# The rotary part of the attention scores in fp32r halves stacked on 128 rows, the queries' second half first, the sample's unit second in a head

## What is computed

```
q = (cq @ w_uq).reshape(B, T, B_HEADS, B_D_NOPE + B_D_ROPE)      # 8 heads, 128 + 64
q_nope, q_rope = q[..., :B_D_NOPE], _rope(q[..., B_D_NOPE:], pos)
q_lat = jnp.einsum('bthn,chn->bthc', q_nope, w_uk)
s = jnp.einsum('bthc,bsc->bhts', ql, kv_lat) + jnp.einsum('bthr,bsr->bhts', qr, kv_rope)
s = s.astype(f32) * ATTN_SCALE
s = jnp.where((k_pos[None, :] <= qp[:, None])[None, None], s, -jnp.inf)
p = jax.nn.softmax(s, axis=-1)
return jnp.einsum('bhts,bsc->bthc', p.astype(kv_lat.dtype), kv_lat)
```

## Time and profile before

| | us |
|---|---|
| three runs | 2582.6, 2584.0, 2591.3; median 2584.0 |
| the profiled execution | 2582.5 |
| its span, first to last instruction | 2580.7 |
| mean granted clock of TensorE over the span | 0.927 |

### The profile page before, as it was taken

The page is one execution under the profiler, slowest core; times in us unless marked ns, Lnnn a source line. Parts: engine busy times, 40 slices in busy tenths (PEclk is TensorE's granted clock), DMA queues, the critical chain, the costliest instruction groups (busy, mean ns, idle before and its releaser), DMA issues. The chain is left out here.

```text
span 2580.7 us, 39435 instructions
## 1 busy us (share of the span) xinstructions
PE 2296.5 (89%) x11502; PEld 1682.2 (65%) x11502; DVE 1370.6 (53%) x2344; ACT 1068.0 (41%) x1818; POOL 309.6 (12%) x390
## 2 busy tenths in 40 slices
PE   5999997878949999999698999999989399999976
PEld 3766665656737788788376666656667287788751
DVE  3213211557975655656384443434369765755647
ACT  2211212533135655655252444544331265654645
POOL 0000001550000100000010334000000010100103
PEclk8999997778969999999899999999999699999985
DMA  6456655536147867876645544222351387866856
GB/s 256 154 202 213 214 187 168 160 99 213 42 156 256 313 217 254 296 265 217 207 157 190 187 159 158 91 93 90 99 205 42 128 302 278 296 243 222 307 183 222
DMA packets 193987, 499.26 MB, mean 193 GB/s; under 512 B 19360, under 2 KB 39297, under 8 KB 187392
## 3 DMA queue, kind: packets, MB, share of 16 engines
q1 hardware_dynamic: 163838, 401.76, 46.0%
q0 software_dynamic: 18992, 66.20, 7.1%
q10 hardware_dynamic: 11058, 30.06, 3.1%
HBM read 432.41 MB, written 68.70 MB: 194 GB/s over the span
## 5 line engine op out<-in xcount | busy, mean ns | idle before, releaser
L1952 DVE TENSOR_TENSOR e_wl<-e_raw,e_wh 128x1024 fp32r<-128x1024 f32 x384 | 449.3, 1219 | 96.4 <-ACT e_wh L1863 95.1
L1863 ACT CAST e_wh<-e_raw 128x1024 fp32r<-128x1024 f32 x384 | 382.3, 1048 | 103.4 <-DMA e_raw<-in_e_up 45.2
L1782 PE MATMUL e_psG<-e_wh,e_xh 128*128 128x512 f32 x784 | 321.5, 410 | 10.2 <-issue 7.4
L1784 PE MATMUL e_psG<-e_wh,e_xl 128*128 128x512 f32 x784 | 311.7, 398 | 0.0
L1783 PE MATMUL e_psG<-e_wl,e_xh 128*128 128x512 f32 x784 | 310.2, 396 | 0.0
L1782 PE MATMUL e_psY<-e_wh,e_hh 128*128 128x512 f32 x392 | 160.8, 410 | 28.2 <-DVE e_hl L1975 28.2
L573 PE MATMUL in_ps<-in_w_upper,in_h_upper 128*128 128x512 f32 (+1 forms) x432 | 174.8, 405 | 3.6 <-issue 3.6
L1782 PEld LDWEIGHTS e_psG<-e_wh,e_xh 128*128 128x128 f32 x784 | 148.7, 190 | 42.6 <-issue 8.2
L1784 PEld LDWEIGHTS e_psG<-e_wh,e_xl 128*128 128x128 f32 x784 | 148.3, 189 | 36.9
L1783 PEld LDWEIGHTS e_psG<-e_wl,e_xh 128*128 128x128 f32 x784 | 149.1, 190 | 32.0
L574 PE MATMUL in_ps<-in_w_lower,in_h_upper 128*128 128x512 f32 (+1 forms) x432 | 169.8, 393 | 0.0
(11 more groups left out here) (574 smaller groups left out, 4241.5 us busy)
## 6 DMA issues: line engine op xcount, KB each, us to landing
e_raw<-in_e_gate SPq DMA_DIRECT2D x32, 2048.0 KB, 11.8
e_raw<-in_e_up SPq DMA_DIRECT2D x32, 2048.0 KB, 9.3
e_raw<-in_e_down SPq DMA_DIRECT2D x32, 2048.0 KB
x<-in_ada_w SPq DMA_DIRECT2D x40, 1024.0 KB, 5.3
yrows<-e_y ACTq DMA_DIRECT2D x49, 512.0 KB, 7.9
x<-in_cache SPq DMA_DIRECT2D x64, 320.0 KB, 3.4
a_pages<-in_cache SPq DMA_DIRECT2D x64, 320.0 KB, 3.4
qkvo<-in_out SPq DMA_DIRECT2D x48, 256.0 KB, 2.0
```

What stands on the lines that cost most here:

```text
L1782: T.matmul(out, upper[:, k, :], wh[:, z, cols], start=k == 0, stop=False)
L1784: mm = T.matmul(out, lower[:, k, :], wh[:, z, cols], start=False, stop=k == PIECES * n - 1)
L1863: S.copy(wh[:, z, c * PC:(c + 1) * PC], raw[:, z, c * PC:(c + 1) * PC]).then_inc(s_hi[z], 1)
L1952: V.tensor_tensor(wl[:, z, at], raw[:, z, at], wh[:, z, at].bitcast(F32), ALU.subtract).then_inc(s_lo[z], 1)
```

## The change

The rotary queries and keys are split into an upper part in fp32r and the rest, a lower part in fp32r. For one of the two heads (`qr[z]`) the tile of 128 rows holds the upper part of the head's queries in its own 64 rows and the lower part in the other 64; `krh` holds the upper part of the keys in both halves of the rows. One matmul of 128 rows gives upper times upper and lower times upper, a second of 64 rows gives upper times the keys' lower part `krl`. `ORDER` changes at two places. The halves of the queries are made in the other order (`step`: r = 0 is now the queries 512 to 1023), and `scores` of tile 0 waits only for r = 0, that of block 0 for r = 1. `turn_heads` gives way to `upper_heads` (ACT), `lower_heads` (DVE) and `lower_heads` (ACT). The storage of some tiles is shared: `w_nope` with its lower part, `w_rope` with its lower part, `krl` with the keys, the sums of the rotary queries with the sample's columns of `mixT`.

```
-    ORDER = (4, 0, 7, None, 6, 1, None, 2, 5, 3)
+    ORDER = (4, None, 7, 0, 6, 1, None, 2, 5, 3)
...
+        krh = sb("kr_upper", [P, SEQ], F32R)
+        krl = nc.alloc_sbuf_tensor_at("a_kr_lower", [P, SEQ], F32R, offset=g.krT_at)
...
-        qr = [sb("qr", [P, SEQ]), sb("qr_turned", [P, SEQ])]
+        qx = nc.alloc_sbuf_tensor_at("a_qr_cosines", [P, SEQ], F32, offset=nc.sbuf_base)
+        qr = [sb("qr_even", [P, SEQ], F32R), sb("qr_odd", [P, SEQ], F32R)]
+        rotated = g.mixT[:, :, SEQ:N]
...
+        def step(r):
+
+            return slice((1 - r) * HALF, (2 - r) * HALF)
...
             def query_product(out, r, high, low):
-                c = slice(r * HALF, (r + 1) * HALF)
+                c = step(r)
...
                     if t == 0:
                         pe.wait_ge(s_ja, 6 * h + 4)
-                        pe.wait_ge(s_qb, 2 * pair + 2)
+                        pe.wait_ge(s_kl, 1)
+                        pe.wait_ge(s_qb, 2 * pair + 1)
...
+                    if i == 0:
+                        pe.wait_ge(s_qb, 2 * pair + 2)
...
+                        own = slice(64 * par2, 64 * par2 + 64)
                         for a in range(parts):
-
-                            mm = T.matmul(psS[:, at + a, 0:w], qr[(a + par2) % 2][64 * a:64 * a + 64, q],
-                                          g.krT[64 * a:64 * a + 64, a * w:(a + 1) * w], start=False, stop=True)
+                            T.matmul(psS[:, at + a, 0:w], qr[par2][:, q], krh[:, a * w:(a + 1) * w], start=False, stop=False)
+                        for a in range(parts):
+                            mm = T.matmul(psS[:, at + a, 0:w], qr[par2][own, q], krl[own, a * w:(a + 1) * w],
+                                          start=False, stop=True)
...
-            def turn_heads(pair, r):
+            def upper_heads(pair, r):
                 act.wait_ge(s_qr, 2 * pair + r + 1)
-                for a in range(2):
-                    S.copy(qr[1][64 * a:64 * a + 64, r * HALF:(r + 1) * HALF],
-                           qr[0][64 - 64 * a:128 - 64 * a, r * HALF:(r + 1) * HALF])
+                for z in range(2):
+                    half = slice(64 * z, 64 * z + 64)
+                    S.copy(by_head(qr[z][half, step(r)]), rotated[half])
+                act.drain()
+                act.sem_inc(s_qh, 1)
+
+            def lower_heads(pair, r):
+                act.wait_ge(s_ql, 2 * pair + r + 1)
+                for z in range(2):
+                    half, other = slice(64 * z, 64 * z + 64), slice(64 - 64 * z, 128 - 64 * z)
+                    S.copy(by_head(qr[z][other, step(r)]), rotated[half])
                 act.drain()
                 act.sem_inc(s_qb, 1)
...
                         if t == 9:
                             if par2:
-                                turn_heads(pair + 1, 0)
+                                upper_heads(pair + 1, 0)
                                 swap_halves(pair + 1, 1)
+                                lower_heads(pair + 1, 0)
                             keys(pair + par2, 1 - par2)
                             if par2:
-                                turn_heads(pair + 1, 1)
+                                upper_heads(pair + 1, 1)
+                                lower_heads(pair + 1, 1)
...
                     split(0, 0)
+                    S.copy(krh[:], g.krT[:, 0:SEQ]).then_inc(s_kh, 1)
             queries(0, 0, 0)
             swap_halves(0, 0)
-            turn_heads(0, 0)
+            upper_heads(0, 0)
             act.wait_ge(s_pq, 1)
             S.copy(qnS[:].rearrange("p h t -> p (h t)"), psP[:, 0:4, :].rearrange("p a t -> p (a t)")).then_inc(s_pn, 1)
+            lower_heads(0, 0)
             queries(0, 0, 1)
             swap_halves(0, 1)
-            turn_heads(0, 1)
+            upper_heads(0, 1)
+            lower_heads(0, 1)
...
             def add_halves(pair, r):
-                cols = slice(r * HALF, (r + 1) * HALF)
                 v.drain()
                 v.wait_ge(s_swap, 2 * pair + r + 1)
-                V.tensor_tensor(qr[0][:, cols], qr[0][:, cols], swap[:], ALU.add).then_inc(s_qr, 1)
-                v.drain()
+                v.wait_ge(s_qb, 2 * pair + r)
+                V.tensor_tensor(rotated, by_head(qx[:, step(r)]), by_head(swap[:]), ALU.add).then_inc(s_qr, 1)
+                v.drain()
+
+            def lower_heads(pair, r):
+                v.wait_ge(s_qh, 2 * pair + r + 1)
+                for z in range(2):
+                    half = slice(64 * z, 64 * z + 64)
+                    V.tensor_tensor(rotated[half], rotated[half], by_head(qr[z][half, step(r)]).bitcast(F32), ALU.subtract)
+                v.drain()
+                v.sem_inc(s_ql, 1)
...
                             if t == 9:
                                 rotate(pair + 1, 1)
+                                lower_heads(pair + 1, 0)
                                 add_halves(pair + 1, 1)
+                                lower_heads(pair + 1, 1)
```

More of the change, by code:

```diff
@@ L2867, in stage_attend @@
         pT = g.x[:, 7:9, :].rearrange("p a (j t) -> p a j t", j=PT)
-        wn, wr, wk = sb("w_nope", [P, 4, P]), sb("w_rope", [P, 4, P]), sb("wk", [P, 2, NOPE])
-        wnh, wnl = sb("w_nope_upper", [P, 4, P], F32R), sb("w_nope_lower", [P, 4, P], F32R)
-        wrh, wrl = sb("w_rope_upper", [P, 4, P], F32R), sb("w_rope_lower", [P, 4, P], F32R)
+        wk = sb("wk", [P, 2, NOPE])
+        wnh, wrh = sb("w_nope_upper", [P, 4, P], F32R), sb("w_rope_upper", [P, 4, P], F32R)
+        wn = nc.alloc_sbuf_tensor_at("a_w_nope", [P, 4, P], F32, offset=nc.sbuf_base)
+        wnl = sb("w_nope_lower", [P, 4, P], F32R)
+        wr = nc.alloc_sbuf_tensor_at("a_w_rope", [P, 4, P], F32, offset=nc.sbuf_base)
+        wrl = sb("w_rope_lower", [P, 4, P], F32R)
+        krh = sb("kr_upper", [P, SEQ], F32R)
+        krl = nc.alloc_sbuf_tensor_at("a_kr_lower", [P, SEQ], F32R, offset=g.krT_at)
         wkT, wv = sb("wkT", [P, KVR]), sb("wv", [P, 2, DV])
@@ L2893, in stage_attend @@
         psO = ctx.enter_context(nc.psum_tensor("a_psO", [P, HALF], F32))
+        s_kh, s_kl, s_qh, s_ql = (sem(x) for x in ("kr_upper", "kr_lower", "q_rope_upper", "q_rope_lower"))
         s_wr, s_wrh, s_wrl, s_sin, s_qb = (sem(x) for x in (
@@ L2912, in stage_attend, with by_head @@
         block = ctx.enter_context(nc.Block())
+        def step(r):
+            return slice((1 - r) * HALF, (2 - r) * HALF)
+        def by_head(a):
+            return a.rearrange("p (h t) -> p h t", h=H)
         def rows(z):
@@ L3290, in queries @@
                 act.wait_ge(s_job, nope_job(pair, par2, r))
-                S.copy(qn[:, r * HALF:(r + 1) * HALF], psS[:, 2 * par2 + (r if par2 else 0), :]).then_inc(s_ja, 1)
+                S.copy(qn[:, step(r)], psS[:, 2 * par2 + (r if par2 else 0), :]).then_inc(s_ja, 1)
             def swap_halves(pair, r):
@@ L3428, in rotate @@
             def rotate(pair, r):
-                cols = slice(r * HALF, (r + 1) * HALF)
+                cols = step(r)
                 v.wait_ge(s_job, jobs_before(pair, 0) + 2 * r + 2)
                 V.tensor_tensor(prod[:], psS[:, 1, :], sinT[:, cols], ALU.mult).then_inc(s_sin, 1)
-                V.tensor_tensor(qr[0][:, cols], psS[:, 1, :], cosT[:, cols], ALU.mult).then_inc(s_jv, 1)
+                V.tensor_tensor(qx[:, cols], psS[:, 1, :], cosT[:, cols], ALU.mult).then_inc(s_jv, 1)
             def add_halves(pair, r):
-                cols = slice(r * HALF, (r + 1) * HALF)
                 v.drain()
                 v.wait_ge(s_swap, 2 * pair + r + 1)
-                V.tensor_tensor(qr[0][:, cols], qr[0][:, cols], swap[:], ALU.add).then_inc(s_qr, 1)
+                v.wait_ge(s_qb, 2 * pair + r)
+                V.tensor_tensor(rotated, by_head(qx[:, step(r)]), by_head(swap[:]), ALU.add).then_inc(s_qr, 1)
                 v.drain()
+            def lower_heads(pair, r):
[5 more added lines that the diff above has]
+                v.sem_inc(s_ql, 1)
             def head(pair, par2, more=True):
@@ L3536, in head @@
                                 rotate(pair + 1, 1)
+                                lower_heads(pair + 1, 0)
                                 add_halves(pair + 1, 1)
+                                lower_heads(pair + 1, 1)
             lower(0, 0)
             v.wait_ge(s_c, 48)
+            v.wait_ge(s_kh, 1)
+            V.tensor_tensor(krl[:], g.krT[:, 0:SEQ], krh[:].bitcast(F32), ALU.subtract).then_inc(s_kl, 1)
             rotate(0, 0)
             add_halves(0, 0)
+            lower_heads(0, 0)
             v.wait_ge(s_pq, 1)
@@ L3766, in build @@
                 g.latT = asb("latT", [P, 2, N])
+                g.krT_at = -(-nc.sbuf_base // 32) * 32
                 g.krT = asb("krT", [P, N])
```

## The result

The changed kernel takes **2601.7 us** (median of 12 runs, 2591.9 to 2607.1), the one before 2584.9 (12 runs, 2579.4 to 2593.8): a ratio of 1.0053, 95% interval 1.0038 to 1.0068. The forecast was 2597.5, slower. The profiled execution of after spans 2597.9 us, that of before 2580.7.

A forecast was written before the change was run, and what follows sets the result against it. PE, busy 417 of 436 us, was taken to bound the attention, so only its instructions' cost and its waits count. The terms summed to +13.4 us on 2582.5, so 2595.9, and a median of 2597.5 us, range 2588 to 2609.

The forecast's parts named there:

- rope products: Rotary matmuls of the scores on PE: +0.15 per two-part block, up to 0.31 less per one-part block; -0.4 us in all.
- T1: Transposes of tile 1 wait for DVE's normalise behind block 7's maximum: 0.85 a head, +6.8 us.
- O2: Outputs of tile 2 (block 7) no longer wait for ACT's copy of block 0's output: -0.96 a head, -7.6 us.
- O4: Outputs of tile 4 (block 6) wait for ACT's copy of block 0's output: +0.7 a head, +5.6 us.
- T7 and O6: Late in the head, tile 7's transposes and tile 6's outputs wait for DVE and ACT on block 5: +1.2 us.
- pairs' ends: Three times, longer cast and subtraction chains delay block 4's scores and the values' copies: 0.6 each, +1.8 us.
- ahead of the loop: Before the heads, the cast and subtraction chain runs uncovered and PE waits for `qS`: +4.3 us of idle PE.
- clock behind it: Behind the idle PE ahead of the heads, the granted clock falls to half for about 3.5 us: +1.7 us.
- rival A: No load exposed at the change from fp32 to fp32r (-5.8), and the clock does not fall (-1.7): 2590; chance 0.15.
- Rival D: Tile 1's transposes meet no wait, because DVE gets to their normalise earlier than its order says: 2590.7 us; chance 0.08.
- B: Scores: the switch to 64 rows, about 0.39 per tile, falls away with fp32r: 25 us less, 2572.5; chance 0.07.
- C: Rope part: every fp32r matmul waits for its own load, 0.09 each, 11.5 us more: 2609; chance 0.10.

The follow-up runs named there:

- e1: Kernel before with the new ORDER alone, rope products unchanged: 2590.5 us, ratio 1.0018 to before.
- e4: Changed kernel with tile 1's normalise ahead of tile 2's maximum on DVE: 2593.2 us, ratio 1.0026 to before.
- e2: Changed kernel with the old ORDER: 2596.9 us, ratio 1.0056 to before.
- e5: Changed kernel with ACT's copy of tile 3's output ahead of tile 6's exponentials: 2588.8 us, ratio 1.0012 to before.
- e3: Changed kernel with ACT's work on the queries' second half, ahead of the loop, moved behind the copies of `qS`: 2592.9 us, ratio 1.0031 to before.
- e9: Changed kernel with the second rotary matmul on all 128 rows, adding the product of the lower parts: 2591.2 us, ratio 1.0011 to before.
- e11_keys_first: As e10, with ACT's half swaps for the next pair moved behind the keys' copies in odd heads: 2569.2 us, ratio 0.9948 to before.
- e7: Kernel before with only ACT's copy of block 0's output ahead of block 6's exponentials: 2579.7 us, ratio 0.9981 to before.
- e10: As e6_all, with the second rotary matmul on all 128 rows: 2572.3 us, ratio 0.9952 to before.
- e6_all: Changed kernel with e3, e4 and e5 together, and the second half's casts and subtractions moved into the next head: 2577.9 us, ratio 0.9971 to before.

## Why the prediction was right, point by point

The sign and the range held. The time was 4.2 us above the forecast. That it came so near is luck in part: the term for the rope products was 5.8 us too high, and T1, the clock and DVE's other waits were 7.1 too low together. The steps came out like this, each read in after's profile:

| step | forecast | measured |
|---|---|---|
| rope products | -0.4 | -6.2 |
| T1, new wait | +6.8 | +8.6 |
| O2, wait removed | -7.6 | -7.6 |
| O4, new wait | +5.6 | +5.9 |
| T7 and O6 | +1.2 | +0.2 |
| pairs' ends | +1.8 | +2.3 |
| ahead of the loop | +4.3 | +4.1 |
| clock behind it | +1.7 | +2.8 |
| clock at two more places | 0 | +3.1 |
| DVE's other waits | 0 | +1.1 |
| sum | +13.4 | +14.3 |

The stage grew by 15.6; 1.3 stay unassigned. The rope products are read in the head from 1554 on. Idle time is counted from modelled ends of matmuls, so rows of this size are uncertain by one or two tenths each.

**Rope products: the mis-sized term.** Start to next start, before and after: blocks of two parts 2.01 and 2.04 (block 4), 2.97 and 3.04 (7), 2.55 and 2.61 (6), 2.23 and 2.29 (5), so +0.03 to +0.07 where I had +0.15. Blocks of one part: -0.13, -0.15, -0.39 and -0.33 (blocks 0 to 3) where I had 0, -0.10, -0.21 and -0.31. (The forecast's own terms, +0.60 and -0.62 a head, give -0.2 and not -0.4.) Twelve passes of 512 columns at 2.4 GHz are 2.56 us. Block 7 stood 0.41 above that and now stands 0.48 above it: if the switch to 64 rows costs the same in both types, the change of type costs 0.07, not the 0.15 by which I had the block longer. The mechanism was right (the passes stay four in a block of two parts, fall by two in a block of one, and the switch to 64 rows stays). The sign that I had set, rope parts of 1.2 and 0.74 us from start to start, can't be read: the first upper matmul of block 7 is recorded at 1564.27, 1.42 behind the block's start, before the eight passes ahead of it (1.71) can be over, so only whole blocks compare. In amount, the 5.8 us of rival A's cheap types came out whole, while its other half, a clock that does not fall, is false. The saving did not show in the time: what block 0 and T0 lost came back as T1's wait, and the clock took more than I had given it.

**T1.** DVE's path was right to 0.03 us: T1 starts 2.37 after S2's end (1565.89 to 1568.26), 2.4 forecast. PE's cover was 1.31 instead of 1.54 (T0 0.60 and block 0 0.71, for 0.70 and 0.84), so the wait was 0.99 to 1.13 instead of 0.85. e1 shows it without the stacking (0.97), and e4 takes it away. Rival D, that it would not come, is out.

**O2 and O4.** No row of after waits for ACT ahead of block 7's outputs. O4's waits are 0.70 to 1.08 in seven heads and none in the first, forecast 0.6 to 0.8 in each. e1, e2 and e5 confirm each.

**A pair's end.** The keys' copies come later and cost 2.6 in three times, against the 1.6 in three for the turned heads before; the values' copies are late only once, 1.26, and there one DVE operation took 1.85 instead of 0.69 (below). "The unit hides all but 0.35, without it 2.2" was about the right price: e2 measured 2.2, 2.1 and 0.6 without it.

**The start.** 4.09 us of idle PE, forecast 4.3, and e3 removed it whole. The clock fell, as I took from the earlier trace rows, but stayed down for 6.8 us, 5.5 of them with PE busy instead of 3 to 4, and the first values and scores took 6.48 against 3.70.

**The rivals.** B is false: the switch to 64 rows does not fall away with fp32r. e9 measures it, 0.30 in a block of two parts, where I had inferred 0.39; for fp32 no run measures it alone. The Trainium skill ("TensorEngine Tiling (Array Packing)", Key Properties) has the drain at a change of mode without regard to type; the trace agrees that the change of shape costs time with fp32r too, by the recorded starts 0.10 on entering and 0.20 on leaving. C is false: block 5 and block 2 are both 384 columns wide, with four rope matmuls and with two. They take 2.29 and 1.29, of which twelve and six passes are 1.92 and 0.96. That leaves 0.37 and 0.33, so the two matmuls more cost 0.04 beyond their passes, where C needed 0.09 for each. The rule that a load overlaps a running matmul only in another row group ("TensorE: Matmul & The Clock Gate", Part 3, The mechanism, in the Trainium skill) doesn't describe these rows.

**What I did not foresee** were the two more falls of the clock, at 1738.8 and 1885.6, and DVE operations stretched beside POOL. The fall at 1738.8 comes in e3 too and not in e4, e5 and e9, so it stands in what these three gained beyond their own waits.

## What to carry to other kernels

When PE sets the time, price a reordering by who is late next, engine by engine with the durations of the trace, and treat a saving that lies directly ahead of a wait as lost. A change that comes out slower by known waits is not yet a bad change: four moves in ACT's and DVE's order turned +0.5% into -0.3%, and dropping the 64-row shape made it -0.5%. But try such a move on the old kernel as well: one alone gave -0.2% there. And before a profile's stage is read as the price of an edit, count the falls of the clock in it and look at the heads without one. Doing a little more arithmetic on all rows can be cheaper than entering and leaving a smaller tile, here by 0.30 us in a block of two parts.

## What the runs showed of the hardware

**The clock falls behind short waits, at some places.** In after it fell behind a wait of 1.12 us that ended at 1738.45, in the middle of narrow matmuls; this is the matmul group behind it, 2.34 us for the ten that take 1.28 elsewhere in the head:

```profile
1738.45 0.82 PE L3210 MATMUL a_psP<-c_ident,x 128*128 128x128 f32 x4 [1.12 <-DVEq L3536]
1739.07 2.34 PE L3238 MATMUL a_psO<-x,a_v 128*128 128x128 f32 x10
```

In e3_start it falls at the same place (1739.0, behind 1.13), in e2_old_order behind a wait of 2.12 for the values, in e11_keys_first behind two of 1.15 and 0.56. But the seven like waits of after's other heads brought no fall, nor did 1.41 us at this place in e9_full_rows. The last head's wait of 2.3 us is the same in all twelve kernels: the clock fell at it in seven (after, e2 to e7) and not in five (before, e1, e9, e10, e11). What decides it I can't say. Each of these falls lasted 3.4 us, but 6.8 in e5's last head and at the start; after's two were worth 1.7 and 1.5 us.

**DVE operations stretch beside POOL's.** A 64-row subtraction of 512 columns takes 0.69 us, in the pair's end at 1674 for both of its two. At the pair's end at 1556, where POOL adds in the same microsecond, DVE shows

```profile
1555.95 0.68 DVE L3479 TENSOR_TENSOR mixT<-mixT,a_qr_even 64x512 f32<-64x512 f32 x1 [1.74 <-ACTq L3327]
1556.65 1.85 DVE L3479 TENSOR_TENSOR mixT<-mixT,a_qr_odd 64x512 f32<-64x512 f32 x1
```

and POOL

```profile
1556.67 1.28 POOL L3049 TENSOR_TENSOR mixT<-mixT 128x512 f32<-128x512 f32 x1
```

The DVE operation that starts with POOL's takes 1.16 longer, and 1.28 is POOL's whole time; it ends 0.55 behind POOL's. In e6_all the same happened to the operations at 1550.12 (1.80) and 1558.10 (1.67), each beside a POOL addition. The values' copies, and the wait of 1.26 for them, stand behind the one shown. In the attention of the twelve profiles, 35 such DVE operations of 512 columns, with two inputs in SBUF, overlap an addition of POOL. In 21 the DVE operation ends 0.55 or 0.56 behind POOL's, whenever it began. In the other 14 DVE began first and took its 0.69, and where it began 0.01 to 0.16 ahead, POOL's took 1.65 to 1.83 instead of 1.27. So one of the two waits for the other. No run took POOL's additions away: the cause is read from these times and not tested by an experiment. The Trainium skill ("GPSIMD Engine Reference", Specifications) says that the two engines share their SBUF interfaces, with contention for a DVE instruction that reads two inputs from SBUF. These are such instructions, and the trace agrees with it; how much they stretch, 1.0 to 1.2 us in the three named here, is the trace's.
